# The opening of a two-layer decoder trunk, taken in two halves of features

## The reference

```
c_act = silu(c)
mod = c_act @ w_ada[l] + b_ada[l]            # six pieces of 1024: sh1, sc1, gt1, sh2, sc2, gt2
h = x * (1 + sc1) + sh1
y = hybrid_mixer(h, positions, w_in[l], ...) # one projection, rotary embedding, two attention groups, projection
x = layer_norm(ALPHA * x + (1 + gt1) * y)
h = x * (1 + sc2) + sh2
x = layer_norm(ALPHA * x + (1 + gt2) * swiglu(h))
```

## Time and profile before

| | |
|---|---|
| median of 3 runs | 1276.03 us (1275.62 to 1276.37) |
| the profiled execution, its own time | 1276.25 us |
| its span in the trace | 1274.6 us |
| PE busy | 1235.8 us, 97% of the span |
| DVE busy | 801.5 us, 63% |
| ACT busy | 510.5 us, 40% |
| POOL busy | 274.2 us, 22% |
| HBM read | 155.31 MB |

### The profile page before, as it was taken

The page is one execution under the profiler, slowest core; times in us unless marked ns, Lnnn a source line. Parts: engine busy times, 40 slices in busy tenths (PEclk is TensorE's granted clock), DMA queues, the critical chain, the costliest instruction groups (busy, mean ns, idle before and its releaser), DMA issues. The chain is left out here.

```text
span 1274.6 us, 18347 instructions
## 1 busy us (share of the span) xinstructions
PE 1235.8 (97%) x6394; PEld 1031.6 (81%) x6394; DVE 801.5 (63%) x1400; ACT 510.5 (40%) x1027; POOL 274.2 (22%) x281
## 2 busy tenths in 40 slices
PE   6999989999999999999999999999999999999997
PEld 5778876889888888888888688778988888888886
DVE  6889997677777764333676699856733355433338
ACT  3555568345232212222145466862643321222220
POOL 4027236600111010000007367570000000000000
PEclk9999999999999999999999999999999999999999
DMA  9672012334878554222523120112232223332211
GB/s 358 240 270 79 33 51 67 132 116 150 279 264 270 193 168 175 90 93 98 171 94 117 66 67 2 37 63 84 75 124 99 97 101 132 99 98 89 94 65 66
DMA packets 44850, 158.30 MB, mean 124 GB/s; under 512 B 5872, under 2 KB 5872, under 8 KB 44784
## 3 DMA queue, kind: packets, MB, share of 16 engines
q1 hardware_dynamic: 30528, 109.07, 24.8%
q0 software_dynamic: 12960, 47.19, 10.9%
q10 hardware_dynamic: 1296, 1.17, 0.3%
HBM read 155.31 MB, written 2.10 MB: 123 GB/s over the span
## 5 line engine op out<-in xcount | busy, mean ns | idle before, releaser
L631 PE MATMUL bank<-hT_hi,w_hi 128*128 128x512 f32 x640 | 249.5, 390 | 0.0
L633 PE MATMUL bank<-hT_hi,w_lo 128*128 128x512 f32 x640 | 249.0, 389 | 0.0
L632 PE MATMUL bank<-hT_lo,w_hi 128*128 128x512 f32 x640 | 249.0, 389 | 0.0
L1967 DVE TENSOR_TENSOR w_lo<-w_raw,w_hi 128x1024 fp32r<-128x1024 f32 x88 | 107.9, 1226 | 147.0 <-ACT w_hi L1434 147.0
L1280 ACT ACTIVATE w_hi<-w_raw 128x1024 fp32r<-128x1024 f32 x96 | 100.7, 1062 | 202.8 <-PE bank L633 189.0
L1434 ACT ACTIVATE w_hi<-w_raw 128x1024 fp32r<-128x1024 f32 x88 | 93.0, 1057 | 161.1 <-PE bank L633 155.8
L631 PE MATMUL bank<-w_hi,hT_hi 128*128 128x512 f32 (+2 forms) x392 | 148.1, 378 | 2.9 <-ACT pq L1316 2.0
L1544 DVE TENSOR_TENSOR w_lo<-w_raw,w_hi 128x1024 fp32r<-128x1024 f32 x88 | 114.1, 1310 | 53.6 <-ACT w_hi L1280 52.2
L633 PE MATMUL bank<-w_hi,hT_lo 128*128 128x512 f32 (+2 forms) x392 | 142.6, 364 | 0.0
L632 PE MATMUL bank<-w_lo,hT_hi 128*128 128x512 f32 (+2 forms) x392 | 142.3, 363 | 0.0
L633 PEld LDWEIGHTS bank<-hT_hi,w_lo 128*128 128x128 f32 x640 | 120.1, 188 | 25.3
(11 more groups left out here) (207 smaller groups left out, 2199.5 us busy)
## 6 DMA issues: line engine op xcount, KB each, us to landing
w_raw<-in_weights SPq DMA_DIRECT2D x184, 512.0 KB, 3.5
ada_w<-in_w_ada POOLq DMA_DIRECT2D x80, 512.0 KB, 5.2
ada_w<-in_w_ada SPq DMA_DIRECT2D x4, 512.0 KB, 6.6
qT<-in_w_ada SPq DMA_DIRECT2D x4, 512.0 KB, 10.0
xs<-in_x SPq DMA_DIRECT2D x4, 512.0 KB, 15.4
g_row<-in_ln_row POOLq DMA_DIRECT2D x4, 512.0 KB, 5.2
b_row<-in_ln_row POOLq DMA_DIRECT2D x4, 512.0 KB, 6.1
trunk_out<-xs SPq DMA_DIRECT2D x8, 256.0 KB, 2.1
```

What stands on the lines that cost most here:

```text
L631: pe.matmul(dst, a_hi, b_hi, start=first, stop=False)
L632: pe.matmul(dst, a_hi, b_lo, start=False, stop=False)
L633: return pe.matmul(dst, a_lo, b_hi, start=False, stop=last)
L1967: nc.vector.tensor_tensor(w_lo[:, s, :], w_raw[:, s, :], w_hi[:, s, :].bitcast(F32), ALU.subtract).then_inc(lo_ready, 1)
```

## The change

The first modulation pieces, x's columns and chunk 0's products are taken in two halves of the feature axis: columns 0 to 511 (`EARLY`, four blocks of 128, `KE` = 4) and columns 512 to 1023 (`LATE`).

- SP issues the left halves of the sixteen row blocks, then piece 0, x tile 0, piece 1, the other three x tiles, the right halves of the sixteen row blocks, and pieces 2 and 3.
- ACT, POOL and DVE scale and add the left halves only. DVE takes ten of the row blocks, ACT and POOL six (nine and seven before). PE's dummies are 4, 6, 2 and 3 (11 and 6 before). One PSUM bank is read for each sum.
- Early rows: scale and shift for columns 0 to 511, x's tiles transposed and scaled in four blocks of 128 columns, high and low halves of that half, and the 48 products of chunk 0 with pieces 0 and 1, all four tiles.
- Late rows: the same for the right halves, with the work cut the other way: PE transposes one block of 128 columns of all four tiles into one bank, ACT and DVE scale such banks, four operations of 512 columns in all. The sums of the right halves stand on PE behind the early products and three of the four transposes. Then come the 48 products with pieces 2 and 3.
- `rope_tables`, the sine and `rope_signs` stand on DVE and ACT behind the late rows and behind the conversion of piece 4 (piece 5 on ACT); their intermediate values lie in `scores` (SBUF) instead of two PSUM banks.

```diff
-SUM_FIRST = ((1, 3, 5, 7), (8, 9, 10))
-VECTOR_FIRST = ((0, 2, 4, 6), (11, 12, 13, 14, 15))
+SUM_FIRST = ((1, 3, 6), (8, 9, 11))
+VECTOR_FIRST = ((0, 2, 4, 5, 7), (10, 12, 13, 14, 15))
+KE = 4
+KH = KE // 2
+EARLY = KE * P
+LATE = slice(EARLY, D_MODEL)
...
             for n in range(2 * KD):
-                sp.dma_start(first_ada[n], w_ada[n // KD, n % KD]).then_inc(ada_first_in[n], 16)
+                sp.dma_start(first_ada[n][:, 0:EARLY], w_ada[n // KD, n % KD][:, 0:EARLY])\
+                    .then_inc(ada_first_in[n], 16)
...
+            load_w(0)
             load_x(0)
-            load_w(0)
             load_w(1)
             load_x(1)
+            load_x(2)
+            load_x(3)
+            for n in range(2 * KD):
+                sp.dma_start(first_ada[n][:, LATE], w_ada[n // KD, n % KD][:, LATE]).then_inc(ada_late_in[n], 16)
             load_w(2)
-            load_x(2)
             load_w(3)
-            load_x(3)
...
+            def late_mod():
+                for vector in (False, True):
+                    for g in range(2):
+                        if vector:
+                            pe.wait_ge(late_sum, 5 * (g + 1))
+                        else:
+                            pe.wait_ge(ada_summed, 4 + 2 * (g + 1))
...
+                        for k in range(KE, KD):
+                            m = pe.matmul(late_column(g, k, 64), part[:, k * P:(k + 1) * P], ones[:, 0:64],
...
+            def open_first():
...
+                early = range(KE // CK[0])
+                pe.wait_ge(h_hi, at_tile(0, 0))
+                pe.wait_ge(hi_ready, converted(0, p0))
+                pairs(0, 0, hT_hi, w_hi)
+                early_transpose(1)
+                pe.wait_ge(lo_ready, converted(0, p0))
+                pairs(0, 0, hT_hi, w_lo)
...
+                for t in range(1, T):
+                    pe.wait_ge(h_hi, at_tile(0, t))
+                    for j in early:
+                        pairs(t, j, hT_hi, w_hi)
+                    if t == 1:
+                        early_transpose(T - 1)
+                    pe.wait_ge(h_lo, at_tile(0, t))
+                    for j in early:
+                        pairs(t, j, hT_lo, w_hi)
+                        m = pairs(t, j, hT_hi, w_lo)
+                        if t == T - 1:
+                            m.then_inc(piece_used, 1)
...
+                for k in range(KE, KD - 1):
+                    late_transpose(k)
+                late_mod()
+                pe.wait_ge(late_taken, 2)
+                late_transpose(KD - 1)
+                j = KE // CK[0]
+                pe.wait_ge(late_hi, 1)
+                pe.wait_ge(hi_ready, converted(0, p0 + j))
+                for t in range(T):
+                    pairs(t, j, hT_hi, w_hi)
...
-            keep_clock(11)
+            keep_clock(4)
             first_mod(0, True, True)
             first_mod(0, False, False)
             keep_clock(6)
             first_mod(1, False, True)
+            keep_clock(2)
             first_mod(1, True, False)
-            pe.wait_ge(rope_table, 2)
-            transpose_x(0, 0, 4)
-            pe.wait_ge(mod_taken, 2)
-            transpose_x(0, 1, 4)
+            early_transpose(0)
+            keep_clock(3)
...
 # ACT
-            act.wait_ge(rope_angle, 1)
-            nc.scalar.activation(angles[:, 1, 0:256], bank[5][:, 0:2 * P], ACT.Sin).then_inc(rope_table, 1)
             convert(0, 1)
-            build_h(0, 0, 4, 0)
+            build_early(0, 1)
             convert(0, 2)
             for t in range(1, T):
-                build_h(0, t, 4, (None, 3, 4, 4)[t])
+                build_early(t, 2)
+            scale_late(0)
+            scale_late(1)
+            convert(0, 3)
+            build_late(0)
+            build_late(1)
+            convert(0, C0P[1] + 2)
+            act.wait_ge(rope_angle, 1)
+            nc.scalar.activation(angles[:, 1, 0:256], scores[:, 2 * P:4 * P], ACT.Sin).then_inc(rope_table, 1)
...
 # DVE
-            take_mod(0, 2)
+            take_early()
+            first_coefficients(0, KE, coef_ready)
+            scale_early(0)
+            convert(0, 1)
+            split_early(0)
...
+            split_early(T - 1)
+            late_vector(0)
+            late_vector(1)
+            take_late()
+            first_coefficients(KE, KD, late_coef)
+            scale_late(0)
+            scale_late(1)
+            split_late(0)
+            convert(0, 3)
+            split_late(1)
+            convert(0, C0P[1] + 1)
+            dve.wait_ge(pos_in, 16 * 2)
+            rope_tables()
+            step(nc.vector.tensor_scalar(nsink[:], nsink[:], -1.0, None, ALU.mult))
             rope_signs()
...
                 if l == 0:
                     for t in range(2):
                         rope_direct(t)
-                    convert(l, C0P[1] + 1)
                     ada_group(2, 0, 2)
```

More of the change, by code:

```diff
@@ L205, in build_trunk @@
         ada_first_in = [sem(f"ada_first_in{i}") for i in range(2 * KD)]
+        ada_late_in = [sem(f"ada_late_in{i}") for i in range(2 * KD)]
         ada_in = [sem(f"ada_in{i}") for i in range(RING)]
@@ L551, in _ @@
             summed = 0
[L552 to L560, removed]
+            for part, cols in enumerate((slice(0, EARLY), LATE)):
+                for g in range(2):
+                    first, total = SUM_FIRST[g][:2]
+                    for i, n in enumerate(SUM_FIRST[g][1:]):
+                        pool.wait_ge(ada_scaled, 6 * part + 3 * g + i + 2)
+                        if i > 0:
+                            pool.wait_ge(ada_summed, summed)
+                        nc.gpsimd.tensor_tensor(first_ada[total][:, cols], first_ada[total][:, cols],
+                                                first_ada[n if i else first][:, cols], ALU.add)\
+                            .then_inc(ada_summed, 1)
+                        summed += 1
             for l in range(DEPTH):
@@ L1557, in first_vector @@
                 for i, n in enumerate(VECTOR_FIRST[g]):
-                    if (g, i) == (0, 1):
-                        dve.wait_ge(pos_in, 16 * 2)
-                        rope_tables()
                     dve.wait_ge(ada_first_in[n], 16)
[L1562 to L1575, removed]
+                    part = bank[0][:]
@@ new lines, in first_vector @@
+                    out = ada_acc[:, g, 0:EARLY] if n == VECTOR_FIRST[g][-1] else part
+                    c = cc[:, 1, n % KD:n % KD + 1]
+                    dve.wait_ge(ada_half, 5 * g + i)
+                    if i == 0:
+                        m = nc.vector.tensor_scalar(out, first_ada[n][:, 0:EARLY], c, None, ALU.mult)
+                    else:
+                        m = nc.vector.scalar_tensor_tensor(out=out, in0=first_ada[n][:, 0:EARLY], scalar=c,
+                                                           in1=part, op0=ALU.mult, op1=ALU.add)
@@ new lines, in first_vector, with late_vector @@
+                    m.then_inc(ada_half, 1)
+            def late_vector(g):
+                acc = ada_acc[:, g, LATE]
+                for i, n in enumerate(VECTOR_FIRST[g]):
+                    c = cc[:, 1, n % KD:n % KD + 1]
+                    dve.wait_ge(ada_late_in[n], 16)
+                    if i == 0:
+                        m = nc.vector.tensor_scalar(acc, first_ada[n][:, LATE], c, None, ALU.mult)
+                    else:
+                        dve.wait_ge(late_sum, 5 * g + i)
+                        m = nc.vector.scalar_tensor_tensor(out=acc, in0=first_ada[n][:, LATE], scalar=c, in1=acc,
+                                                           op0=ALU.mult, op1=ALU.add)
+                    m.then_inc(late_sum, 1)
@@ new lines, in scale_early @@
+            def scale_early(t):
+                dve.wait_ge(x_transposed, at_tile(0, t))
+                parts_free(dve, 0, t)
+                for k in range(KH):
+                    m = nc.vector.tensor_scalar(h_part(0, t)[:, k * P:(k + 1) * P],
+                                                bank[4 + 2 * (t % 2)][:, k * P:(k + 1) * P],
+                                                hcoef[:, 0, 0, k:k + 1], hcoef[:, 0, 1, k:k + 1], ALU.mult, ALU.add)
+                m.then_inc(h_scaled_dve, 1)
@@ L1892, in rope_tables @@
                 step(m)
-                turns = bank[4][:, P:3 * P]
+                turns = scores[:, 0:2 * P]
                 nc.vector.tensor_scalar(turns[:, 0:128], ang, 1.0 / two_pi, None, ALU.mult)
```

226 lines of the change are left out of this document (172 added, 54 removed).

## The result

The new kernel took 1281.28 us, the median of six runs (1279.57 to 1282.00); the kernel before took 1275.69 in the runs beside them (1275.36 to 1276.37). The ratio is 1.0041, with a 95% interval of 1.0028 to 1.0054: slower by 5.6 us, where 1275.6 was forecast and 1280.5 was the upper end of the range. The profiled execution took 1282.0 us, its span is 1280.1.

What follows compares the result with a forecast made beforehand. DVE's list was taken to set chunk 1's end: D = 47.9 + 4.1 + 0.5 + 0.65, written 53.2, so the gain 53.65 - 53.2 = 0.45 us gives 1275.6 against the median; 8-in-10 range 1271.8 to 1280.5.

Steps and rivals of the forecast that it cites:

- D: Time at which DVE starts to rotate the first tile: 48.90 us before, forecast 53.2; the gain is 53.65 - D.
- Late sums: Right-half sums behind PE's early products: DVE's ten products, 0.79 us each, end at 38.3; sums end at 39.4.
- the cover: DVE's ten late products end at 38.3, needed at 38.4: 0.1 us to spare, beyond which lateness goes into D.
- the stall in chunk 1: In the first projection's second chunk PE waits 3.1 us for piece 5's low half, about 1.6 before piece 6.
- angles, sine and signs: Rotary tables moved onto DVE's list before the rotation: angles 4.1 us, sine with waits 0.5, sign tables 0.65.
- late rows to angles: After the late sums at 39.4: coefficients, scaling, high half to 42.15, then five DVE operations of 1.15, to 47.9.
- half loads: Half-width row loads cost nothing more than bytes; late halves land by 33.0 us; 0.4 kept for the range.
- DVE's 3.55 us of slack: DVE's idle time before 89.09, ahead of the index heads: used up exactly, so no further loss behind chunk 1.
- the clock stays low: Slower rival: PE's early-sum list all at 1.2 GHz, D 58.8, loss 5.15 us, 1281.2; chance 0.19.
- dear half loads: Slower rival: half loads cost what whole ones do, late rows land near 53 us, D 68.4, 1290.8; chance 0.05.
- the earlier list: Faster rival: PE at upper level from its first dummy, early sums end at 18.1, gain 2.35 us; chance 0.27.

## Why the prediction was wrong, point by point

**The rule for the time was right.** The prediction said that DVE's list sets the end of chunk 1 and that the gain is 53.65 - D. Then the index scores must begin at 87.31 + D - 53.65. Before and after they begin here:

```profile
87.31 2.21 PE L926 MATMUL bank<-kiT,qT 64*128 64x512 f32 x8 [0.69 <-ACT kiT L1346]
```
```profile
91.66 2.21 PE L1034 MATMUL bank<-kiT,qT 64*128 64x512 f32 x8 [0.69 <-ACT kiT L1456]
```

In the profiled executions the rule gives 91.65 for the new kernel (91.66 in the trace), 86.40 without POOL's adds (86.42), 88.88 with the sums in PSUM (88.88), 90.23 with the dummies (90.23) and 83.04 with PE kept busy (83.03); in the three other runs where DVE waits for PE ahead of the rotation it is right within 0.05. Behind that point the kernel before takes 1276.25 - 87.31 = 1188.94 us, and eight of the ten changed kernels take 1188.9 to 1189.3. The new kernel takes 1190.34, and the one with the angles between the early sums 1190.51.

**The step that failed is *Late sums*:** "ten products of late rows, 0.79 each" from 30.4, "so just hidden; the cover is 0.1 us", and "on POOL four adds of half a row lie under the early products". The price was taken from the earlier trace rows, an operation that adds up in PSUM, for one that adds up in SBUF. Alone that is right: 7.75 us for ten without POOL's adds. But the adds run at the same time, and the ten took 11.29: POOL's interference was a term put at nothing. With 0.55 us of later start they end at 42.24 instead of 38.3. The cover was gone after 0.1 us, as the text itself said, and the rest went into D. POOL's adds were looked at for what PE needs of them and not for what they do to DVE. The trace of the kernel before had rows with the price, further on. DVE's low half of a piece reads two operands from SBUF and takes 1.22 us in the earlier trace rows; beside POOL's rotation it took 2.17, and POOL's next operation 2.16, where the one before it took 1.31 (DVE's row, then POOL's):

```profile
97.69 2.17 DVE L1544 TENSOR_TENSOR w_lo<-w_raw,w_hi 128x1024 fp32r<-128x1024 f32 x1
```
```profile
97.47 1.31 POOL L412 TENSOR_TENSOR scratch<-pq,cos_t 128x512 f32<-128x512 f32 x1
98.86 2.16 POOL L417 TENSOR_TENSOR pq<-scratch 128x512 f32<-128x512 f32 x1
```

The adaLN product with its accumulator in SBUF, the very kind that the change put beside POOL, took 1.83 us at 168.70 beside two of POOL's operations, and 1.27 to 1.29 in its 34 other places. The Trainium skill states the rule, on the page "SBUF — State Buffer", section "Who interferes with whom": a DVE instruction with two SBUF inputs contends with a GpSimd instruction that reads SBUF, one in a two-port mode contends with GpSimd as well, and whichever issues first holds the shared ports for its whole length, while one with at most one SBUF input outside those modes does not contend. The runs agree as far as they go: 0.75 to 1.59 us with the accumulator in SBUF, 0.48 to 1.49 for the product with a scalar, 0.75 with the accumulator in PSUM; that the product with a scalar is in such a mode no run shows.

**A second loss stands behind it.** PE waited 0.68 and 1.72 us in its late sums, and its clock fell; the last sum took 1.84 us instead of the 1.10 that it takes with the dummies, 0.74 of D. The prediction feared a fall of the clock, but in the early sums and after the stall in chunk 1. In chunk 1 PE stalled for 0.24 and 1.29 us, not for 3.1 and 1.6, because it came there 7.5 us late itself. Where it came nearer to its forecast time, the stall was there in one piece, 2.90 us with the sums in PSUM and 2.92 with the dummies, and behind it the clock did fall (0.50 from 66 to 68 us in the row of the run with the dummies). It cost nothing: in both runs the index scores began where the rule puts them. Nor did PE's lateness cost anything by itself, as the run with dummies shows.

**The sum of D.** DVE read the late sums 4.77 us later than forecast (44.17 for 39.4). That is 0.55 for the start of the late products (PE's first dummies began at 9.05 and not at 8.3, and the first product was 0.83 late), 3.39 for POOL (11.29 for 7.9), 0.93 for the last sum and its reading (1.93 for 1.0, most of it the clock), less the 0.1 of cover. Behind that, late rows and angles together were as forecast within 0.02: 4.79, from 53.2 to 57.99. Sizes that held: angles, sine and signs took 5.20 (5.25 forecast); late rows to angles 8.62 (8.5); half loads moved at 385 to 420 GB/s from 8 to 38 us, so that they cost little more than their bytes. The last late row landed at 35.71 and not by 33.0, but no late product of DVE's waited for a row.

**The remaining 1.4 us** is a new wait of DVE: 1.59 us at 80.51 for a row of w_ada, whose fetch was issued at 73.23 and landed 7.19 us later (4.71 in the run with the dummies). The prediction had DVE's 3.55 us of slack before the index heads used up exactly, so such a wait counts in full. It shows in one other execution (1.24 us, with the angles between the early sums) and in none of the rest. Which other transfer held the row up stays open. 4.8 + 1.4 is the 6.2 us between the forecast for the profiled execution, 1275.8, and its 1282.0. Without that wait the forecast and 4.8 would make 1280.4, just inside the stated range.

**Of the rivals,** "the clock stays low" came nearest in time (1281.2), but not in its place or its mechanism; dear half loads didn't happen. Of the earlier list, the prediction's reason was right that PE's own dummies and not the rows set the early sums' end: with four dummies less the first product came 1.9 us earlier.

## What to carry to other kernels

When work of two engines is newly laid side by side, look at where each operand lies before taking a duration from a row: on DVE the same operation on the same data was dear or free beside POOL by whether its accumulator lay in SBUF or in PSUM. When a step is moved onto a list that sets the end, its whole length counts, less the slack behind it, and the waits that the list still has are the places to put it. An engine that doesn't lead can be given microseconds for nothing; shorten the list that leads, and the same microseconds count.

## What the runs showed of the hardware that was not expected

An add of POOL and a product of DVE on 128x512 f32, both wholly in SBUF, cost each other 0.8 to 1.0 us on DVE's side and 0.3 to 0.6 on POOL's (1.53 to 1.84 instead of 1.27), and even an operation of 0.23 us took 1.24. PE's granted clock fell to the 1.2 GHz level behind waits of 0.68 and 1.72 us in one execution, of 0.95 and 1.58 in another, of 0.96 and 1.92 in a third and of 0.32 and 1.92 in a fourth, and behind single waits of 2.90 and 2.92, but did not behind 0.66 and 1.92 us; these rows don't tell what decides. With the waits filled by products of a zero matrix the clock stayed at 1.00 from 36 to 53 us of the profiled execution, and the runs lie within 0.44 us of each other (1271.95 to 1272.39) where those of the new kernel spread over 2.4.
